# Attention of layers 1 and 2 in blocks: scores, values and transposes of three head pairs side by side, once a cycle

## The reference, cut to what matters

```python
# layer 1 (chunked_mixer)
q = (h @ w_q).reshape(B, n_c, CHUNK, B_HEADS, B_HEAD_DIM)
s = jnp.einsum('bnqhd,bnkhd->bnhqk', q, k_band) * (B_HEAD_DIM ** -0.5) + bias
p = jax.nn.softmax(s, axis=-1)
o = jnp.einsum('bnhqk,bnkhd->bnqhd', p, v_band).reshape(B, S, B_HEADS * B_HEAD_DIM)
return o @ w_o
# layer 2, heads 8 to 15 (stick_breaking_attention)
log_later = lax.cumsum(log_keep, axis=3, reverse=True) - log_keep
a = jnp.where(past, jnp.exp(log_beta + log_later), 0.0)
return jnp.einsum('bhqk,bhkd->bhqd', a.astype(v.dtype), v)
```

## Time and profile before

| | |
|---|---|
| median of three runs | 961.36 us |
| the profiled execution, timed | 960.99 us |
| its span (first to last instruction) | 959.1 us |
| TensorE busy | 944.2 us, 98% of the span |
| VectorE, ScalarE, GpSimd busy | 718.9, 543.6, 17.8 us |
| DMA | 195.62 MB, mean 204 GB/s |

### The profile page before, as it was taken

One profiled execution on the slowest core, in us unless ns is written; L12 is line 12 of the kernel. 1 busy time (PEld: TensorE's weight loads), 2 busy tenths in 40 slices (PEclk: granted clock), 3 DMA queues, 4 the chain that ended last, 5 costly groups with the idle time before them and its releaser, 6 DMA issues.

```text
span 959.1 us, 18737 instructions
## 1 busy us (share of the span) xinstructions
PE 944.2 (98%) x7890; PEld 911.9 (95%) x7890; DVE 718.9 (75%) x1332; ACT 543.6 (57%) x845; POOL 17.8 (2%) x51
## 2 busy tenths in 40 slices
PE   9999999999999999999999999999999999999997
PEld 9989999999998988899999998998999999999996
DVE  7875897787569777799888789655656789888653
ACT  7755654444447366565444554556756576766542
POOL 0000000000000000000000000000320000000000
PEclk9999999999999999999999999999999999999999
DMA  9645487667736734268768892653344636555621
GB/s 341 231 169 206 166 281 249 233 251 270 256 134 220 263 132 139 83 224 314 295 227 290 317 329 75 258 176 133 107 143 147 220 132 220 183 213 179 217 89 44
DMA packets 28259, 195.62 MB, mean 204 GB/s; under 512 B 3216, under 2 KB 3600, under 8 KB 5264
## 3 DMA queue, kind: packets, MB, share of 16 engines
q1 hardware_dynamic: 28176, 194.43, 57.3%
HBM read 192.98 MB, written 1.05 MB: 202 GB/s over the span
## 4 chain that ended last, share of the span: by engine, by line
PE 93%; ACT 3%; DVE 2%; DMA 1%; issue 1%; SPq 0%; POOL 0%; DVEq 0%; ACTq 0%
PE bank L548 26%; PE bank L549 25%; PE bank L554 25%; PE bank L750 2%; PE bank L776 2%; PE bank L592 2%; PE bank L603 2%; PE bank L597 1%; PE bank L760 1%; PE bank L631 1%; PE bank L637 1%; PE bank L632 1%; PE bank L669 1%; PE bank L675 1%; PE bank L670 1%; DMA s_front<-in_front 1%
## 5 line engine op out<-in xcount | busy, mean ns | idle before, releaser
L1507 DVE TENSOR_TENSOR s_wlo<-s_raw,s_whi 128x512 fp32r<-128x512 f32 (+1 forms) x354 | 364.4, 1070 | 121.9 <-ACT s_whi L1017 121.7
L1017 ACT ACTIVATE s_whi<-s_raw 128x1024 fp32r<-128x1024 f32 (+2 forms) x226 | 299.5, 1353 | 193.6 <-PE bank L554 187.3
L548 PE MATMUL bank<-s_hh,s_whi 128*128 128x256 f32 x1392 | 390.2, 280 | 1.3 <-DVE s_wlo L1507 1.0
L549 PE MATMUL bank<-s_hl,s_whi 128*128 128x256 f32 x1392 | 384.8, 276 | 0.0
L554 PE MATMUL bank<-s_hh,s_wlo 128*128 128x256 f32 x1383 | 382.2, 276 | 0.0
L548 PEld LDWEIGHTS bank<-s_hh,s_whi 128*128 128x128 f32 x1392 | 261.4, 188 | 6.6 <-issue 4.2
L549 PEld LDWEIGHTS bank<-s_hl,s_whi 128*128 128x128 f32 x1392 | 261.5, 188 | 0.1
L554 PEld LDWEIGHTS bank<-s_hh,s_wlo 128*128 128x128 f32 x1383 | 259.7, 188 | 0.0
L548 PE MATMUL bank<-s_ph,s_whi 128*128 128x256 f32 x528 | 145.9, 276 | 0.0
L549 PE MATMUL bank<-s_pl,s_whi 128*128 128x256 f32 x528 | 145.7, 276 | 0.0
L554 PE MATMUL bank<-s_ph,s_wlo 128*128 128x256 f32 x525 | 144.9, 276 | 0.0
(11 more groups left out here) (274 smaller groups left out, 1288.6 us busy)
## 6 DMA issues: line engine op xcount, KB each, us to landing
s_raw<-in_gu SPq DMA_DIRECT2D x44, 1024.0 KB, 5.0
s_raw<-in_dn SPq DMA_DIRECT2D x33, 1024.0 KB, 4.9
s_raw<-in_wada SPq DMA_DIRECT2D x24, 1024.0 KB, 5.2
s_raw<-in_up SPq DMA_DIRECT2D x22, 1024.0 KB, 4.9
s_raw<-in_wo SPq DMA_DIRECT2D x8, 1024.0 KB, 4.9
s_raw<-in_win_g SPq DMA_DIRECT2D x8, 1024.0 KB, 4.9
s_raw<-in_mla SPq DMA_DIRECT2D x4, 1024.0 KB, 13.9
s_raw<-in_wkv_v SPq DMA_DIRECT2D x4, 1024.0 KB, 5.7
```

The costliest lines, as they stand in the source:

```text
L548: e.matmul(out, hi, xh[:, k, :], start=first, stop=False, skip_group_check=True)
L549: e.matmul(out, hi, xl[:, k, :], start=False, stop=False, skip_group_check=True)
L1017: e.activation(whi[w % SPLIT][:, at], src, ACT.Copy).then_inc(S.hi.tick((w, c0)), 1)
L1507: e.tensor_tensor(wlo[s][:, at], src, whi[s][:, at].bitcast(F32), ALU.subtract).then_inc(S.lo.tick((i, j), (i, "all")), 1)
```

## The change

`_order1` and `_order2` no longer call `_mixed`. A new function `_in_blocks` puts the steps at fixed places: in front of unit `blocks[c]` stand the scores of pair c, the values of pair c-2 and all six transposes of pair c-1, then the chunk of pair c-2 and the exponentials of pair c; the scaling of pair c stands five units on. `turn_both` issues the six transposes of layer 1 together, into banks 6 and 7, with the head order kept; the copy of the second head is split in two because it lies in two banks. The values of layer 1 move to the second half of bank 7. One split low-part matmul moves from unit 102 to unit 86 of `win_g`. Layer 0 is left as it is.

```diff
+BLOCKS1 = (21, 31, 41, 52, 62, 72, 83, 93, 106, 113)
+BLOCKS2 = (21, 31, 41, 52, 64, 81, 98, 115, 132, 147)
+
+def _in_blocks(units, blocks, pairs, soft):
+    plan = {}
+    def at(n, *steps):
+        plan.setdefault(n, []).extend(steps)
+    for c, n in enumerate(blocks):
+        if c < pairs:
+            at(n, ("scores" if c < soft else "sticks", c))
+        if 0 <= c - 2 < pairs:
+            at(n, ("values", c - 2))
+        if 0 <= c - 1 < soft:
+            at(n, ("turn", (c - 1, 0)), ("turn", (c - 1, 1)))
+        elif soft <= c - 1 < pairs:
+            at(n, ("sums", c - 1))
+            at(n + 4, ("stick", c - 1))
+        if 0 <= c - 2 < pairs:
+            at(n if c - 2 < soft else n + 2, ("chunk", c - 2))
+        if c < soft:
+            at(n, ("exp", c))
+            at(n + 5, ("scale", c))
+        elif c < pairs:
+            at(n + 9, ("keep", c))
+    for n, unit in enumerate(units):
+        yield from plan.get(n, ())
+        yield unit
...
 def _order1():
-    return _mixed(_units("wq1") + _units("wo1"), _soft_steps(range(8)), {"wq1": 0.35, "wo1": 0.35},
-                  lambda p: ("wq1", 16 * (p // 2) + 15), "wo1")
+    return _in_blocks(_units("wq1") + _units("wo1"), BLOCKS1, 8, 8)
...
+            def turn_both(s, A, p):
+                take(6, S.soft, (s, "turned", p, 1))
+                bank_of[s, "turn", p] = (6, 7)
+                if p >= 1:
+                    q.wait_ge(S.soft, (s, "turned", p - 1, 1))
+                else:
+                    q.wait_ge(*freed[7])
+                for i in range(6):
+                    a = i // 3
+                    q.wait_ge(S.score, (s, p, "scaled", a))
+                    m = e.transpose(banks[6 + i // 4][:, i % 4 * P:(i % 4 + 1) * P],
+                                    A.S[p % 2][:, a, i % 3 * P:(i % 3 + 1) * P], ident[:, :])
+                    if i % 3 == 2:
+                        m.then_inc(S.attn.tick((s, "turn", p, a)), 1)
...
             def turned(s, A, p, a):
-                bank = banks[bank_of[s, "turn", p, a]]
-                q.wait_ge(S.attn, (s, "turn", p, a))
+                q.wait_ge(S.attn, (s, "turn", p, 1 if (s, "turn", p) in bank_of else a))
                 if p >= 2:
                     q.wait_ge(S.attn, (s, "values", p - 2))
+                if (s, "turn", p) in bank_of:
+                    first, second = (banks[b] for b in bank_of[s, "turn", p])
+                    to = A.PT[p % 2][:, a, :]
+                    if a == 0:
+                        m = e.activation(to, first[:, 0:384], ACT.Copy)
+                    else:
+                        e.activation(to[:, 0:P], first[:, 384:512], ACT.Copy)
+                        m = e.activation(to[:, P:384], second[:, 0:T], ACT.Copy)
+                    m.then_inc(S.soft.tick((s, "turned", p, a)), 1)
+                    return
```

More of the change, by code:

```diff
@@ L109 @@
 HALVED = {("wo0", 36): (0,), ("gu0", 0): (1,), ("gu0", 4): (4,), ("gu0", 8): (4,), ("wkv_k", 0): (1,), ("wo1", 52): (0,), ("gu1", 0): (1,), ("gu1", 4): (2,),
-          ("gu1", 8): (1,), ("win_k", 0): (1,), ("win_g", 102): (0,), ("wbr", 0): (1,), ("wout", 0): (1,), ("up2", 0): (1,),
+          ("gu1", 8): (1,), ("win_k", 0): (1,), ("win_g", 86): (0,), ("wbr", 0): (1,), ("wout", 0): (1,), ("up2", 0): (1,),
           ("up2", 8): (1,)}
@@ L223, in _order0 @@
     return _mixed(units, _soft_steps(range(4)), PACE0, lambda p: units[PAIR0[p]], "wo0", 2, AFTER0)
+BLOCKS1 = (21, 31, 41, 52, 62, 72, 83, 93, 106, 113)
[24 more added lines that the diff above has]
+        yield unit
 def _order1():
-    return _mixed(_units("wq1") + _units("wo1"), _soft_steps(range(8)), {"wq1": 0.35, "wo1": 0.35},
-                  lambda p: ("wq1", 16 * (p // 2) + 15), "wo1")
+    return _in_blocks(_units("wq1") + _units("wo1"), BLOCKS1, 8, 8)
 def _order2():
-    return _mixed(_units("win_q") + _units("win_g"), itertools.chain(_soft_steps(range(4)), _stick_steps(range(4, 8))),
-                  {"win_q": 0.3, "win_g": 0.2}, lambda p: ("win_q", 16 * (p // 2) + 15), None)
+    return _in_blocks(_units("win_q") + _units("win_g"), BLOCKS2, 8, 4)
 class Signal:
@@ L417, in tile_out, with values_out @@
             return banks[bank_of[name, j - j % 2]][:, (j % 2) * T:(j % 2 + 1) * T]
+        def values_out(s, p, n):
+            at = T if s == "o1" else 0
+            return banks[bank_of[s, "values", p]][:, at:at + n * T]
         def pair(bank):
@@ L761, in turn, with values @@
                 m.then_inc(S.attn.tick((s, "turn", p, a)), 1)
-            def values(s, A, p, dv, probs, v_event, p_signal, p_event, b):
-                bank = take(b, S.xlo, (s, p))
+            def turn_both(s, A, p):
[12 more added lines that the diff above has]
+                        m.then_inc(S.attn.tick((s, "turn", p, a)), 1)
+            def values(s, A, p, dv, probs, v_event, p_signal, p_event, b, at=0):
+                bank = take(b, S.xlo, (s, p))[:, at:512]
                 bank_of[s, "values", p] = b
@@ L898, in tensor_program @@
                     scores("o1", i, half_parts(A1, i), (4, 5))
-                elif step == "turn":
-                    turn("o1", A1, *i, 6 if i[0] < 2 else (5, 6)[i[1]])
+                elif step == "turn" and i[1] == 0:
+                    turn_both("o1", A1, i[0])
                 elif step == "values":
-                    values("o1", A1, i, 64, A1.PT[i % 2], ("wkv_v", i // 4, 1), S.soft, ("o1", "turned", i, 1), 7)
+                    values("o1", A1, i, 64, A1.PT[i % 2], ("wkv_v", i // 4, 1), S.soft, ("o1", "turned", i, 1), 7, T)
             sums("y1", 4, late=[(3, sqb[1][:, j, :]) for j in range(2)])
@@ L1065, in turned @@
             def turned(s, A, p, a):
-                bank = banks[bank_of[s, "turn", p, a]]
-                q.wait_ge(S.attn, (s, "turn", p, a))
+                q.wait_ge(S.attn, (s, "turn", p, 1 if (s, "turn", p) in bank_of else a))
                 if p >= 2:
                     q.wait_ge(S.attn, (s, "values", p - 2))
+                if (s, "turn", p) in bank_of:
[8 more added lines that the diff above has]
+                    return
+                bank = banks[bank_of[s, "turn", p, a]]
                 e.activation(A.PT[p % 2][:, a, :], bank[:, 0:384], ACT.Copy).then_inc(S.soft.tick((s, "turned", p, a)), 1)
             def chunk(s, A, p, n):
-                bank = banks[bank_of[s, "values", p]]
+                bank = values_out(s, p, n)
                 q.wait_ge(S.attn, (s, "values", p))
-                e.activation(A.oh[:, n * p:n * (p + 1), :], bank[:, 0:n * T], ACT.Copy).then_inc(S.xhi.tick((s, p)), 1)
+                e.activation(A.oh[:, n * p:n * (p + 1), :], bank, ACT.Copy).then_inc(S.xhi.tick((s, p)), 1)
             def tokens_out(name, g, V, R=None):
@@ L1584, in chunk @@
             def chunk(s, A, p, n):
-                bank = banks[bank_of[s, "values", p]]
                 q.wait_ge(S.xhi, (s, p))
                 to = slice(n * p, n * (p + 1))
-                src = pair(bank) if n == 2 else bank[:, 0:T].rearrange("p (a b) -> p a b", a=1)
+                src = values_out(s, p, n).rearrange("p (a b) -> p a b", a=n)
                 e.tensor_tensor(A.ol[:, to, :], src, A.oh[:, to, :].bitcast(F32), ALU.subtract).then_inc(
```

## The result

The changed kernel takes 969.7 us, the median of four executions (969.44 to 969.86), beside 961.28 for the kernel before in the same rounds: a ratio of 1.0089, with a 95% interval of 1.0077 to 1.0101. It is slower, as forecast, but by 8.4 us where 5.3 were forecast, and it lies outside the range. The profiled execution of the change took 969.44 us with a span of 967.6, that of before 960.99.

A forecast was written before the change was run, and what follows sets the result against it. TensorE, busy 98% at full clock, bounds the kernel. Layer 1 +5.4 us (7.0 new waits less 0.6 old waits and 1.0 saved), layer 2 -0.1: 961.36 + 5.3 = 966.7 us, range 962.8 to 968.8.

The forecast's parts named there:

- Wait of pair 1: Layer 1, T0 to T1: the softmax chain takes 6.5 us, so TensorE waits 0.5 at pair 1's transposes.
- Pair 3: Layer 1, T2 to T3: VectorE gets to the bias late, the chain takes 7.9 us, wait 1.9.
- Pair 4: Layer 1, T3 to T4: the chain with one low part takes 6.2 us, wait 0.2.
- Pair 6: Layer 1, T5 to T6: the chain from VectorE's bias step takes 7.25 us, wait 1.3.
- Pair 7: Layer 1, last transposes: TensorE waits 2.5 us for the scaling of pair 7.
- Second heads: Layer 1, five waits: second head scaled 0.46 behind the first, three transposes take 0.34; 0.6 us in all.
- Clock: Rival, chance 0.04: granted clock falls to 1.2 of 2.4 GHz from T7 to the stage's end, some 9 us; 976 us.
- Old waits: Waits of TensorE in the kernel before that go away: 0.6 us in layer 1, 0.6 in layer 2.
- Own work: TensorE enters fewer float32 blocks, 0.20 us each: 1.0 us saved in layer 1, 1.6 in layer 2.
- T6 to T7 ... Wait 2.5: Layer 1, transposes of pair 6 to pair 7: chain with the 128x2048 piece takes 8.6 us against 6.17, wait 2.5.
- my bounds of 0.25 and 0.34: Cost in us of a turn of three transposes inside a block; the prediction took 0.34.
- The faster rival: Chance 0.10: the softmax chain ends within 5.99 us, the two-block distance, so only savings stay; 957 us.

The follow-up runs named there:

- the last experiment: The change with the scaling two units behind its block instead of five, one unit for pair 3, in both layers: 957.19 us, ratio 0.9959.
- the select moved: The change with GpSimd's mask select over bias2 made to wait for the transposes of pair 7: 966.46 us, ratio 1.0054.
- wait filled: The change with 18 additional matmuls that nobody reads, put on TensorE right ahead of the transposes of pair 7: 967.01 us, ratio 1.0065.
- layer 1 alone: Layer 1 as in the change, layer 2 in the order of before: 969.17 us, ratio 1.0085 against the kernel before.
- the one-unit kernel: The change with the scaling one unit behind its block instead of five, in both layers: 961.68 us, ratio 1.0005.
- The first with the early scaling: The change with the scaling two units behind its block instead of five, in both layers: 958.87 us, ratio 0.9977.

## Why the prediction was wrong, point by point

The first unit of layer 1 and the first of the feed-forward part behind it bound the layer. Before, of the change, and of the last experiment:

```profile
326.38 0.28 PE L548 MATMUL bank<-s_qh,s_whi 128*128 128x256 f32 x1
...
398.69 0.38 PE L592 MATMUL bank<-s_hh,s_whi 128*128 128x256 f32 x1 [0.75 <-ACT s_hh L1230]
```

```profile
326.37 0.28 PE L584 MATMUL bank<-s_qh,s_whi 128*128 128x256 f32 x1
...
406.95 0.39 PE L628 MATMUL bank<-s_hh,s_whi 128*128 128x256 f32 x1 [0.75 <-ACT s_hh L1292]
```

```profile
326.59 0.28 PE L584 MATMUL bank<-s_qh,s_whi 128*128 128x256 f32 x1
...
396.46 0.38 PE L628 MATMUL bank<-s_hh,s_whi 128*128 128x256 f32 x1 [0.75 <-ACT s_hh L1292]
```

72.3, 80.6 and 69.9 us. By terms, forecast and measured, for layer 1:

| Term | Forecast | Measured | From |
|---|---|---|---|
| Wait of pair 1 | 0.5 | 0.6 | trace of the change |
| Pair 3 | 1.9 | 1.7 | " |
| Pair 4 | 0.2 | 0.3 | " |
| Pair 6 | 1.3 | 1.1 | " |
| Pair 7 | 2.5 | 4.1 | 2.6 of it with the select moved |
| Second heads | 0.6 | 0.6 | five times 1.00 less 0.88 |
| Clock | 0 | 2.7 | 969.7 less 967.0, wait filled |
| Old waits | -0.6 | -0.6 | |
| Own work | -1.0 | -1.8 | 69.9 less 72.3, less the old waits |
| Sum | +5.4 | +8.7 | the layer itself: +8.3, alone +8.1 |

- **The failed step** is "T6 to T7 ... Wait 2.5", with what the sum puts behind that wait. Two things were wrong in it. The scaling counts with 0.8 until its first head, read from a pair that nothing disturbs; GpSimd's select lay over it, and the wait was 4.1. And the clock behind the wait counts with nothing; it cost 2.7. Either alone would have left the time in the range: 967.0 with the wait filled, 966.5 with the select moved, where the mean clock is the lower one in three of five executions only. The longer scaling wasn't a matter of an unknown price: it stands in the trace of before at this very pair, 2.69 us under a select of 2.09. It cost nothing there, because TensorE had other work until the scaling was done. In the change TensorE stands at the transposes before the scaling has begun, and the prediction says of GpSimd's queue only that it keeps its instructions. It does; what they cost is another matter. The Trainium skill, SBUF — State Buffer, section Who interferes with whom, states that a tensor_scalar of VectorE can take the port pair that it shares with GpSimd, and that the later of two such instructions is held until the first has ended. The trace agrees: the select runs from 387.23 to 389.48, the first of the multiplies begins 0.57 us into it, and the longest of them takes 1.76 us, to 389.56. By the rule the first multiply ends with the select, 1.5 us later than its 0.27 us alone would have it; the time at which the select meets the scaling is the trace's, not the rule's.
- **The clock** was a rival with 0.04, put at +9 over the main case; it came true in its mechanism, with +2.7. What was wrong is the extent: it fell from about 389 to 396, and only the six transposes and the seven units in front of the last block (21 matmuls), not 22 units and the block, ran at half speed. What I weighed against it, that the waits of before left the clock alone, says nothing of a wait ten times as long; even the 2.5 that it forecast was six times as long. The Trainium skill, TensorE: Matmul & The Clock Gate, Part 1, has an idle TensorE's clock halved, and the filled wait agrees: 1.00 with it, 0.50 without. What the Trainium skill, TensorE: Matmul & The Clock Gate, Part 4, states, that transposes don't count as busy work, isn't borne out as a cause here: in the last experiment the same blocks of six transposes, without waits, leave the clock at 1.00 in the whole stretch, and so does the block of pair 7 behind the filled wait.
- **Right** was the mechanism and the size of the other waits: which pairs wait and which don't (2 and 5 don't), each within 0.25 us, and that nothing covers them. That VectorE's queue order causes them is shown by moving one step in it: from 7.8 us in five waits to 1.5 in one.
- **Own work** was undersized in layer 1 and oversized in layer 2. A block without a wait costs 2.48 us over its units (370.69, the last unit's start, to 373.51, less three matmuls), against 1.86 for scores and values together as forecast, so 0.31 for a turn: between my bounds of 0.25 and 0.34. Sixteen turns at 0.31 instead of the 0.34 that I took give 0.5 of the 0.8 by which layer 1 saved more. Layer 2 came to +0.3: 1.8 of waits and 0.2 of second heads (forecast 0.4) less 0.6 of old waits leave some 1.1 of own savings where 1.6 were forecast. I haven't followed that difference up, and it is no larger than what the ratio of that run can tell (0.9 us to either side).
- **The faster rival** (957, 0.10) names its own condition, that the chain ends within the distance of two blocks, as it does "without weight parts". The last experiment comes close to that: between exponentials and scaling it leaves room for one low part at most, for pair 3 for none, and it takes 957.2.

The terms overshoot the layer's 8.3 by some 0.4, which stays open. Own work was measured in another kernel than the waits, which is a likely place but not shown.

## What to carry to other kernels

When steps of several engines are tied to one place, write out the chain between two such places and look at what else stands in each queue inside it: here not the softmax work made the chain too long but the weight parts inside it; with the select and the clock behind them they cost 8 us. Moving one step ahead by three units turned +8.4 into -2.2, and by four for one pair into -3.6. Then look at the engines whose queues don't change (GpSimd, the transfers) in the trace of before: what they delay there without harm counts once the cover is gone. Take a step's price from its own row, not from that of its like in another pair. And price an idle stretch of TensorE of the lengths seen here (1.7 us and up) above its length, since the clock behind it may be the lower one, in some executions or in all.

## What the hardware showed that I had not expected

- Work of TensorE that goes on at half clock after the wait is over: 389.88 to about 395.5, with 21 unit matmuls at 0.213 us instead of 0.113. All eight executions with the wait of 4.1 us (four of the change, four of layer 1 alone) have the lower mean clock, 0.995 or 0.996.
- The drop is not settled by the length of the wait alone: 1.74 us left the clock full in the profile of the change, 1.73 us took it down in that of the select moved; 2.60 us left it full there, and 3.05 us did in the profile of the one-unit kernel, of whose other executions eight took 961.1 to 962.9 us at a lower mean clock. The kernels whose longest wait is 1.7 to 3.1 us spread over 1.3 to 3 us from one execution to the next. The first with the early scaling, whose longest is 1.5, spreads over 0.7 in eleven executions, all at a mean clock of 0.998 or 0.999, and the last, without such waits, over 0.5.
- The select took 2.25 us where VectorE's low part of 128x2048, with two inputs in SBUF, was still running at its start, and 1.95 us where it ran apart (moved, or in the last experiment). The first multiply was held by the select, which moving it shows. That the select was held by the low part only seems so; I haven't tried it by itself.
